# Two transformer blocks on one core: the first block's gating products, weight halves and conv taps in another order

## The chip, the cores and the metric

The kernel runs on one core of a Trainium2 chip. The metric is the time of one execution on the device in microseconds (us). A core has TensorE (PE in the profile; its weight loads are PEld), VectorE (DVE), ScalarE (ACT), GpSimd (POOL) and SyncE (SP), which here issues the loads of weights. Each engine takes its instructions in the order in which they are written; semaphores join the engines.

## The reference

The input is 1024 tokens of 1024 values, float32. The first block, which the change concerns:

```python
h = rms_norm(x, norm1_g)
u_a, v_a, val_b, gate_b = split(h @ w_in)                  # 4 x 512 columns
v = layer_norm(gelu(v_a)).reshape(1, 8, 128, 4, 128)
mixed = einsum('hts,bcshd->bcthd', tril(sgu_w), v) + sgu_b
a_out = gelu(u_a) * mixed
g = val_b * sigmoid(gate_b)
c = causal depthwise conv of g, 31 taps, + conv_b
b_out = silu(layer_norm(c in 4 groups of 128))
x = x + concat(a_out, b_out) @ w_out
h = rms_norm(x, norm2_g)
x = x + square(relu(h @ w_ff1)) @ w_ff2                    # 4096 wide
return rms_norm(x, final_g)
```

The second block follows: a layer of differential attention, a layer of stick-breaking attention, with their projections. It is the same before and after.

## The kernel before

**Products.** A float32 matrix becomes two float16 halves, a high one (value times a power of two, rounded) and a low one (what the rounding left). A product takes high by high, high by low and low by high: 24 matmuls of 128 x 512 for one bank of PSUM with a sum over 1024, 12 with a sum over 512. Weights come in 42 tiles of 2 MB. Tiles 0 to 3 are `w_in` (val, gate, v, u), 4 and 5 `w_out`, from 6 on the feed-forward layer. Tile i is loaded by SyncE into one raw buffer once tile i-1 is converted (`weight`). ScalarE adds up its absolute values (`total`), GpSimd takes the largest sum over the partitions, VectorE makes the power of two (`factor`, three small operations), ScalarE the high half, VectorE the low half (`convert_low`); `convert` on VectorE is `factor` and `convert_low` in a row, so VectorE waits out ScalarE's high half. Tile 0 takes its peak on VectorE.

**Order.** There is no scheduler: the functions `tensor`, `vector`, `scalar`, `gpsimd`, `sync` are each engine's program. The first block, in n = 0, 1 (halves of the tokens) and m = 0 to 3 (groups of 128 channels):

1. `tokens("ht")` turns the scaled input on TensorE, `tokens_high` and `tokens_low` split it; `tokens("xt")` turns the raw input into `XT`, the residual stream.
2. 16 products of val and gate: all val of n = 0, all gate of n = 0, then for each m val and gate of n = 1. `gate` is a Sigmoid on ScalarE, `glu` the multiplication on VectorE. A group of the convolution needs `glu` of both halves.
3. The convolution: `run_taps(k)` gives VectorE the next k of 120 taps of `taps_order`, each 128 x 1024, four chains of 30, with two chains alternating at first. It is called in portions between VectorE's other work.
4. 8 products v, 8 products u; `bn_stats`, then two passes over V; 8 `sgu` products (each a bias matmul with one row and four 128 x 128 matmuls in float32); VectorE multiplies them by gelu(u) and takes a peak of each half (`gated_peak`). GpSimd, then `power`, `gated_high` on ScalarE and `gated_low` on VectorE follow.
5. Part 0 of the output product (`out_part(0, ...)`, 16 of them, z = 0 to 15), each followed by `out_residual` on VectorE. Between them: `centre`, `centre_sums`, `centre_spread` (the group norm on TensorE), `centre_factor`, `mix_norm`, `mix_silu`, `mix_high`, `mix_lows`.
6. Part 1, 16 products over the convolution's channels; its first product needs group 3 to be through. Then the second norm and the feed-forward layer.

`mix_high` waits for the last tap of all, since its buffer `MH[1]` lies over the convolution's input `G`. In the profile one line stands for a helper: L72 matmul, L75 transpose, L81 activation, L84 copy on ScalarE, L90 copy, L93 `tensor_tensor`, L96 `tensor_scalar`, L101 `scalar_tensor_tensor` (taps, residuals, low halves), L110 reduction, L113 reciprocal, all on VectorE but for the first four.

## Time and profile before

| | us |
|---|---|
| median of 3 runs (2599.11 to 2602.09) | 2599.43 |
| the profiled execution | 2594.74 |
| its span, first to last instruction | 2592.9 |
| TensorE busy | 2361.3 |
| VectorE busy | 1543.2 |
| ScalarE busy | 953.7 |

A profile shows one execution. "Busy" adds up the time in which an engine works. The busy shares are means over the whole span; the first block fills only its first 439 us, which is where the change lies.

### The profile page before, as it was taken

Reading aid. Unit: us, or ns where it says so; the run is one execution under the profiler, and the core shown is the slowest. Engines: PE = TensorE matmul, PEld = TensorE weight load, DVE = VectorE, ACT = ScalarE, POOL = GpSimd, SP = SyncE. Lnnn points to the kernel's source line nnn. Section 1 sums busy time; section 2 is a strip of 40 time slices with the busy share of each in tenths; the row PEclk is TensorE's granted clock in tenths of the full one; section 3 lists DMA queues with packets and bytes.
Section 4 is the critical chain, followed back from the end, with each engine's and each line's share of the span. In section 5 each row is a group of like instructions: output and inputs, shape, how many; then the busy total and the mean of one; then the engine's idle time right before and its main releaser. Section 6 shows DMA issues by size and latency. Waiting matters only on the chain.

```text
span 2592.9 us, 30076 instructions
## 1 busy us (share of the span) xinstructions
PE 2361.3 (91%) x12784; PEld 1249.2 (48%) x12784; DVE 1543.2 (60%) x1979; ACT 953.7 (37%) x1346; POOL 208.2 (8%) x264
## 2 busy tenths in 40 slices
PE   6998659999999999898999967889999998888899
PEld 3444324444444444444444445664444445676764
DVE  5569885564445545577651278974644405988852
ACT  5232223321212212333322166761323214777741
POOL 0000002000000000333320201002000000000000
PEclk9997769999999999999999989999999998999999
DMA  4010000121111011103010000011140200000021
GB/s 172 33 65 33 33 0 1 66 80 51 46 52 65 33 65 38 56 8 130 33 65 33 33 1 1 1 66 65 33 162 14 84 1 33 1 1 1 1 82 49
DMA packets 50321, 115.99 MB, mean 45 GB/s; under 512 B 2384, under 2 KB 7817, under 8 KB 49804
## 3 DMA queue, kind: packets, MB, share of 16 engines
q1 hardware_dynamic: 48452, 105.39, 11.4%
q10 hardware_dynamic: 1736, 8.68, 0.8%
q8 instruction: 101, 1.65, 0.3%
q14 instruction: 32, 0.26, 0.0%
HBM read 101.49 MB, written 12.58 MB: 44 GB/s over the span
## 4 chain that ended last, share of the span: by engine, by line
PE 69%; DVE 19%; ACT 7%; issue 3%; DMA 1%; POOL 1%; SPq 0%; DVEq 0%; POOLq 0%; ACTq 0%
PE PS L72 66%; DVE R L101 7%; ACT RG L81 4%; PE PS L75 3%; DVE R L93 3%; DVE RG L101 2%; DVE RG L107 2%; DVE mx L110 2%; ACT R L81 1%; DVE scl L110 1%; ACT OV L84 1%; DMA RG<-in_a_w_in 1%; DVE RG L93 1%; DVE oss L110 1%; ACT OV L81 0%
## 5 line engine op out<-in xcount | busy, mean ns | idle before, releaser
L72 PE MATMUL PS<-R,RG 128*128 128x512 f16 (+1 forms) x5472 | 1173.0, 376 | 42.0 <-DVE R L101 29.9
L72 PEld LDWEIGHTS PS<-R,RG 128*128 128x128 f16 (+1 forms) x5472 | 544.2, 104 | 667.0 <-issue 58.7
L72 PE MATMUL PS<-RG,R 128*128 128x512 f16 x2880 | 634.2, 381 | 3.8 <-DVE R L101 3.8
L72 PEld LDWEIGHTS PS<-RG,R 128*128 128x128 f16 x2880 | 282.7, 98 | 337.0 <-issue 6.5
L81 ACT ACTIVATE R<-PS,scl 128x512 f32<-128x512 f32 (+1 forms) x200 | 131.0, 686 | 724.9 <-PE PS L72 601.5
L101 DVE SCALAR_TENSOR_TENSOR R<-PS,scl,R 128x512 f32<-128x512 f32 (+1 forms) x216 | 155.1, 746 | 178.4 <-PE PS L72 131.6
L72 PE MATMUL PS<-R,OV 128*128 128x64 f32 (+2 forms) x1456 | 194.4, 286 | 58.5 <-DVE R L93 31.7
L107 DVE TENSOR_TENSOR_SCAN RG<-RG 128x127 f32<-128x127 f32 (+7 forms) x128 | 168.6, 1345 | 108.9 <-ACT RG L81 108.3
L101 DVE SCALAR_TENSOR_TENSOR RG<-RG,scl 128x4096 f16<-128x4096 f32 x42 | 188.6, 4490 | 71.0 <-ACT RG L81 71.0
L72 PEld LDWEIGHTS PS<-R,OV 128*128 128x128 f32 x1456 | 180.6, 199 | 70.1 <-DVE R L93 38.5
L81 ACT ACTIVATE RG<-RG,scl 128x4096 f16<-128x4096 f32 x42 | 155.7, 3708 | 137.7 <-DVE scl L113 137.6
L75 PE MATMUL PS<-ident,RG 128*128 128x128 f32 x864 | 147.9, 288 | 49.6 <-ACT OV L84 23.9
L110 DVE TENSOR_REDUCE scl<-RG 128x1 f32<-128x4096 f32 x35 | 154.5, 4413 | 64.9 <-DMA RG<-in_a_w_in 24.9
L122 POOL PARTITION_ALL_REDUCE scl<-scl x63 | 33.6, 535 | 1752.9 <-DVE scl L110 1357.3
L81 ACT ACTIVATE RG<-PS,scl 128x1024 f32<-128x1024 f32 (+3 forms) x172 | 168.6, 982 | 0.9 <-PE PS L72 0.9
L104 DVE CUSTOM_DVE_ANT_0 R<-R 128x512 f32<-128x512 f32 (+1 forms) x66 | 44.3, 676 | 181.1 <-ACT R L81 180.9
L101 DVE SCALAR_TENSOR_TENSOR R<-R,OV 128x1024 f32<-128x1024 f32 x120 | 150.7, 1279 | 1.9
L84 ACT COPY OV<-PS 128x512 f32<-128x512 f32 (+3 forms) x215 | 110.9, 516 | 106.0 <-PE PS L75 102.0
L72 PE MATMUL PS<-R 64*128 64x512 f16 (+3 forms) x1152 | 124.9, 343 | 22.3 <-ACT RG L81 20.4
L75 PEld LDWEIGHTS PS<-ident,RG 128*128 128x128 f32 x864 | 102.5, 153 | 63.1 <-DVE RG L101 26.6
L81 ACT ACTIVATE RG<-PS,mx,scl 128x128 f32<-128x128 f32 (+7 forms) x128 | 106.0, 839 | 41.8 <-DVE mx L96 41.2
L93 DVE TENSOR_TENSOR R<-PS,R 128x512 f32<-128x512 f32 (+1 forms) x96 | 64.7, 683 | 71.2 <-ACT R L81 46.0
(109 smaller groups left out, 1538.9 us busy)
## 6 DMA issues: line engine op xcount, KB each, us to landing
RG<-in_w_ff SPq DMA_DIRECT2D x16, 2048.0 KB, 8.1
RG<-in_a_w_in SPq DMA_DIRECT2D x8, 2048.0 KB, 8.7
RG<-in_w_in SPq DMA_DIRECT2D x4, 2048.0 KB, 10.0
xspill<-R ACTq DMA_DIRECT2D x2, 4096.0 KB, 16.3
RG<-in_w_kv SPq DMA_DIRECT2D x4, 2048.0 KB, 8.4
RG<-in_b_w_in SPq DMA_DIRECT2D x4, 2048.0 KB, 8.0
R<-in_x SPq DMA_DIRECT2D x8, 512.0 KB, 9.6
RG<-in_w_out SPq DMA_DIRECT2D x2, 2048.0 KB, 7.7
```

The lines of the kernel that those rows point to most:

```text
L72: return self.engine.matmul(*a, **k) if self.engine else Nothing()
L75: return self.engine.transpose(*a) if self.engine else Nothing()
L81: return self.engine.activation(*a, **k) if self.engine else Nothing()
L84: return self.engine.copy(*a) if self.engine else Nothing()
L93: return self.engine.tensor_tensor(*a) if self.engine else Nothing()
L101: return self.engine.scalar_tensor_tensor(out=out, in0=in0, scalar=scalar, in1=in1, op0=op0, op1=op1)
L104: return self.engine.tensor_tensor_reduce(*a) if self.engine else Nothing()
L107: return self.engine.tensor_tensor_scan(*a) if self.engine else Nothing()
L110: return self.engine.tensor_reduce(*a, **k) if self.engine else Nothing()
L122: return self.engine.partition_all_reduce(*a) if self.engine else Nothing()
```

## The change

Eight edits, all in the first block:

- **First tile by halves.** Tile 0's high and low half are each made in two pieces of 2048 columns (`first_high`, `first_low`), between the splits of the tokens; the first product starts on the first piece (`by_half`). `factor(0)` moves ahead of three splits.
- **Group by group.** For each m: gate of n = 0, val of n = 1, gate of n = 1, `glu` of both, then taps. `tokens_raw(0)` moves behind the 16 products, on ScalarE alone; `tokens_raw(1)` and `tokens_scaled(1)` move forward. The Sigmoid's output lies in two other buffers.
- **Factor apart from the low half.** For tiles 1 to 6 `factor(i)` stands some taps or splits ahead of `convert_low(i)`.
- **Taps.** Chain 1 starts after 10 taps of chain 0 instead of 6. 29 taps stand before the v products' statistics (20 before), 50 before the last statistics (42), 65 before the gating multiplications (70), and one tap follows each of the first six of these.
- **Gated scale from sums.** Two reductions on VectorE are replaced by eight `Abs` passes with a sum on ScalarE; one factor serves both halves.
- **Centring earlier.** `centre(0)` and `centre(1)` stand ahead of the output products, `centre(2)` at z = 12.
- **Buffers.** `MH[1]` lies in R2, the squares in R0, and `mix_high` of groups 0 to 2 no longer waits for the last tap.
- `total` writes its unused output into a slot of the weights and waits for that slot.

TensorE, start of the program; L75 are transposes, 128x124 turns the taps, RG holds weights:

```order
-L75 MATMUL PS<-ident,R 128x128 x64
+L75 MATMUL PS<-ident,R 128x128 x32
 L72 MATMUL PS<-R,RG 128x512 x48
 L75 MATMUL PS<-ident,R 128x128 x32
-L72 MATMUL PS<-R,RG 128x512 x72
-L75 MATMUL PS<-ident,R 128x128 x32
-L72 MATMUL PS<-R,RG 128x512 x96
+L72 MATMUL PS<-R,RG 128x512 x24
+L75 MATMUL PS<-ident,R 128x128 x16
+L72 MATMUL PS<-R,RG 128x512 x24
+L75 MATMUL PS<-ident,R 128x128 x16
+L72 MATMUL PS<-R,RG 128x512 x24
```

The raw input's first half (32 transposes) has left the place ahead of the first product.

VectorE, the gating stage; `PS,scl,dg` and `PS,scl,OV` are `glu` of n = 0 and 1, 128x1024 the taps:

```order
+L101 SCALAR_TENSOR_TENSOR R<-PS,scl,dg 128x512 [waits s_bank_act,s_w_scale]
 L90 COPY OV<-PS 128x124 [waits s_bank_full]
-L101 SCALAR_TENSOR_TENSOR R<-PS,scl,R 128x512 [waits s_bank_act,s_bank_dve]
+L101 SCALAR_TENSOR_TENSOR R<-PS,scl,OV 128x512 [waits s_bank_full,s_bank_act,s_bank_dve]
+L96 TENSOR_SCALAR R<-R,OV,cols 128x1024 [waits s_glu]
+L101 SCALAR_TENSOR_TENSOR R<-R,OV 128x1024 [waits s_conv_dve] x3
+L101 SCALAR_TENSOR_TENSOR R<-PS,scl,dg 128x512 [waits s_bank_act]
+L101 SCALAR_TENSOR_TENSOR R<-R,OV 128x1024 [waits s_conv_dve] x7
+L96 TENSOR_SCALAR scl<-scl 128x1 [waits s_w_top]
```

The first tap now stands behind the second `glu`, where before three more `glu` stood ahead of it.

TensorE, behind the last `sgu` product; `R,OV` is centring, `ones,R` sums of squares, `OV,ones` the spread:

```order
-L72 MATMUL PS<-R,RG 128x512 x24
 L72 MATMUL PS<-R,OV 128x512 x4
-L72 MATMUL PS<-R,RG 128x512 x48
-L72 MATMUL PS<-ones,R 128x1 x16
+L72 MATMUL PS<-ones,R 128x1 x8
+L72 MATMUL PS<-R,RG 128x512 x12
+L72 MATMUL PS<-ones,R 128x1 x8
 L72 MATMUL PS<-R,RG 128x512 x36
 L72 MATMUL PS<-OV,ones 128x512 x2
 L72 MATMUL PS<-R,RG 128x512 x24
 L72 MATMUL PS<-OV,ones 128x512 x2
-L72 MATMUL PS<-R,RG 128x512 x60
```

Centring of two groups now comes first; one output product stands between the two groups of sums.

The diff, cut to what the prediction speaks of:

```diff
-        sgt = R2[:, 0:1024].rearrange("p (a n) -> p a n", a=2)
+        sgt = [dg[:, :, :].rearrange("p t q -> p (t q)"), OV[:, 1024:1536]]
...
-        SQC = R2[:, 0:4096].rearrange("p (m n) -> p m n", m=4)
-        MH = [R3[:, 4096 * i:4096 * i + 4096].bitcast(F16).rearrange("p (s k n) -> p s k n", s=2, k=4)
-              for i in range(2)]
+        SQC = R0[:, 0:4096].rearrange("p (m n) -> p m n", m=4)
+        gated_abs = R0[:, 4096:8192].rearrange("p (j n) -> p j n", j=8)
+        gated_sums = mx[:, 16:24]
+        MH = [a.bitcast(F16).rearrange("p (s k n) -> p s k n", s=2, k=4) for a in (R3[:, 0:4096], R2[:, 0:4096])]
+        SQ3 = R3[:, 4096:8192].rearrange("p (k n) -> p k n", k=8)
...
-        taps_order = ([(0, w) for w in range(1, 7)]
-                      + [(m, w) for w in range(1, TAPS - 6) for m, w in ((0, w + 6), (1, w))]
-                      + [(1, w) for w in range(TAPS - 6, TAPS)]
+        taps_order = ([(0, w) for w in range(1, 11)]
+                      + [(m, w) for w in range(1, TAPS - 10) for m, w in ((0, w + 10), (1, w))]
+                      + [(1, w) for w in range(TAPS - 10, TAPS)]
...
+                e.wait_ge(*(sig("weight").at(i, 0) if by_half else sig("weight").at(i)))
...
+                    if by_half and k == 4:
+                        e.wait_ge(*sig("weight").at(i))
...
             tokens_scaled(0)
-            tokens_raw(0)
+            product_t(0, 0, 0, h_rhs, ("val", 0, 0), 0, ready=h_ready("norm1", 0), by_half=True)
+            product_t(0, 1, 0, h_rhs, ("val", 1, 0), 1)
+            tokens_scaled(1)
+            product_t(0, 2, 0, h_rhs, ("val", 2, 0), 2)
+            tokens_raw(1, range(4))
+            product_t(0, 3, 0, h_rhs, ("val", 3, 0), 3)
+            tokens_raw(1, range(4, 8))
+            places = [(4, 5, 6), (7, 0, 4), (5, 1, 6), (7, 2, 0)]
             for m in range(4):
-                if m == 2:
-                    tokens_scaled(1)
-                product_t(0, m, 0, h_rhs, ("val", m, 0), m, ready=h_ready("norm1", 0))
-            for m in range(4):
-                if m == 1:
-                    tokens_raw(1)
-                product_t(1, m, 0, h_rhs, ("gate", m, 0), 4 + m % 2)
-            for m in range(4):
-                product_t(0, m, 1, h_rhs, ("val", m, 1), ready=h_ready("norm1", 1))
+                product_t(1, m, 0, h_rhs, ("gate", m, 0), places[m][0])
                 if m == 0:
...
                     e.transpose(b[:, 0:124], taps_t, ident[0:124, 0:124]).then_inc(*full.up("taps"))
-                product_t(1, m, 1, h_rhs, ("gate", m, 1))
...
+                product_t(0, m, 1, h_rhs, ("val", m, 1), places[m][1], ready=h_ready("norm1", 1))
+                product_t(1, m, 1, h_rhs, ("gate", m, 1), places[m][2])
+            for c in range(3):
...
+            tokens_raw(0)
...
+            centre(0)
+            centre(1)
+            centre_sums(0)
             for z, (n, c, mi) in enumerate(out_order):
-                if z == 2:
-                    centre(0)
-                    centre(1)
+                if z == 1:
+                    centre_sums(1)
+                if z == 4:
+                    centre_spread(0)
                 if z == 6:
-                    centre_sums(0)
-                    centre_sums(1)
-                if z == 9:
-                    centre_spread(0)
-                if z == 11:
                     centre_spread(1)
+                if z == 12:
+                    centre(2)
+                if z == 14:
+                    centre_sums(2)
                 out_part(0, n, c, mi)
-            for mi in (2, 3):
-                centre(mi)
-                centre_sums(mi)
-                centre_spread(mi)
+            centre_spread(2)
+            centre(3)
+            centre_sums(3)
+            centre_spread(3)
...
+            def first_low(j):
+                e.wait_ge(*sig("w_high").at(0, j))
+                s, a = w_slot(0), 2048 * j
+                low_half(s[:, a:a + 2048], s[:, 4096 + a:6144 + a], w_raw(0)[:, a:a + 2048], w_col(0, 2)).then_inc(
+                    *(sig("weight").up(0) if j else sig("weight").up(0, 0)))
...
-            for k in range(4):
+            tokens_low(0, 0)
+            factor(0)
+            tokens_low(0, 1)
+            tokens_low(0, 2)
+            first_low(0)
+            tokens_low(0, 3)
+            tokens_low(0, 4)
+            first_low(1)
+            for k in range(5, 8):
                 tokens_low(0, k)
-            e.wait_ge(*sig("w_top").at(0))
-            power(w_inv(0), w_col(0, 2), w_col(0, 1)).then_inc(*sig("w_factor").up(0))
-            for k in range(4, 8):
-                tokens_low(0, k)
-            convert_low(0)
-            tokens_raw(0)
             tokens_scale(1)
             h_scale(0, "norm1")
-            for k in range(8):
+            for k in range(3):
                 tokens_low(1, k)
-            convert(1)
+            factor(1)
+            for k in range(3, 8):
+                tokens_low(1, k)
+            convert_low(1)
...
             for m in range(4):
                 glu(m, 0)
...
-                if m == 2:
-                    convert(2)
-                    h_scale(2, "norm1")
-            for m in range(4):
                 if m == 0:
                     e.wait_ge(*full.at("taps"))
...
+                if m == 2:
+                    run_taps(1)
+                    convert_low(2)
+                    h_scale(2, "norm1")
+                if m:
+                    run_taps(3 if m == 2 else 7)
+                if m == 1:
+                    factor(2)
                 glu(m, 1)
...
-                run_taps(5)
+                run_taps(2 if m == 3 else 3)
...
+            for t in range(NT):
+                run_taps(0 if t == 3 else 3)
+                if t == 1:
+                    factor(3)
+                if t == 3:
+                    convert_low(3)
+                    h_scale(3, "norm1")
+                if t == 7:
+                    factor(4)
+                if t:
+                    v_stats(t - 1)
+            v_stats(NT - 1)
+            for t in range(NT):
...
+            run_taps(10)
+            factor(5)
+            run_taps(4)
+            convert_low(5)
+            run_taps(1)
...
-            for n in range(2):
-                e.wait_ge(*sig("bank_dve").at("sgu", 3, n))
-                e.tensor_reduce(col(86 + n), MIX[:, 0:4, cols512(n)], AX.XY, ALU.max,
-                                apply_absolute_value=True).then_inc(*sig("gated_peak").up(n))
-            run_taps(2)
-            for n in range(2):
-                e.wait_ge(*sig("gated_top").at(n))
-                power(col(57 + n), col(92 + n), col(90 + n)).then_inc(*sig("gated_factor").up(n))
-            for n in range(2):
-                run_taps(2)
+                    run_taps(1 if h < 3 else 0)
+            run_taps(1)
...
             for z, (n, c, mi) in enumerate(out_order):
-                if z == 3:
-                    convert(6)
+                if z == 0:
+                    gated_lows(1)
+                if z == 2:
+                    centre_factor(0)
+                if z == 4:
+                    mix_norm(0)
+                    centre_factor(1)
+                if z == 5:
+                    factor(6)
+                if z == 6:
+                    mix_norm(1)
                 if z == 8:
-                    centre_factor(0)
+                    convert_low(6)
                 if z == 10:
-                    centre_factor(1)
+                    mix_lows(0)
                 if z == 11:
-                    mix_norm(0)
-                if z == 13:
-                    mix_norm(1)
-                if mi == 0:
-                    out_scale(0, n, c)
+                    mix_lows(1)
+                if mi == 0 and n == 0:
+                    out_scale(0, c)
                 out_residual(0, n, c, mi)
-                run_taps(1 if z in (3, 8, 10, 11, 13) else 2 if z % 2 else 1)
-            run_taps(max(0, 98 - taken[0]))
+                run_taps(0 if z in (2, 4, 6, 8) else 1)
+                if z == 11:
+                    run_taps(max(0, 90 - taken[0]))
             centre_factor(2)
             run_taps(4)
             mix_norm(2)
+            run_taps(6)
+            mix_lows(2)
...
+                if i == 2:
+                    e.wait_ge(*sig("weight").at(1))
+                if 3 <= i < 7:
+                    e.wait_ge(*full.at(*last_product.get(i - 3, ())))
+                out = R3[:, 0:2048].bitcast(F16) if i == 7 else w_slot(i)[:, 0:4096]
...
+            for h in range(4):
+                for n in range(2):
+                    e.wait_ge(*sig("bank_dve").at("sgu", h, n))
+                    e.activation(gated_abs[:, 2 * h + n, :], MIX[:, h, cols512(n)], ACT.Abs,
+                                 accum_out=gated_sums[:, 2 * h + n:2 * h + n + 1]).then_inc(*sig("gated_sum").up(h, n))
...
-            convert(6)
             centre(0)
+            gated_highs(0)
             centre(1)
+            gated_highs(1)
             centre_root(0)
             centre_root(1)
+            total(6)
             mix_silu(0)
+            mix_high(0)
+            convert(6)
             mix_silu(1)
-            centre(2)
-            centre_root(2)
-            mix_silu(2)
-            for mi in range(3):
+            mix_high(1)
+            for mi in (2, 3):
+                centre(mi)
+                centre_root(mi)
+                mix_silu(mi)
                 mix_high(mi)
```

## Rows read from the trace of the kernel before

**Rows 1.** Page part 2: busy tenths of 40 slices of 64.8 us

```profile
PE   6998659999999999898999967889999998888899
PEclk9997769999999999999999989999999998999999
```

**Rows 2.** By stretch: us, busy us of each engine (instructions), clock, DMA

```profile
core 0: us, PE busy (x) PEld busy (x) DVE busy (x) ACT busy (x) POOL busy (x), PEclk, DMA share, GB/s
...
35.00:135.49 100.49, 98.74 (x460) 46.62 (x460) 49.18 (x64) 25.54 (x27) 0.80 (x2) 0.97 0.09 34
135.49:218.46 82.97, 82.97 (x385) 37.46 (x383) 66.04 (x93) 31.31 (x26) 1.82 (x3) 1.00 0.15 51
218.46:249.40 30.94, 29.01 (x81) 16.64 (x80) 26.77 (x24) 10.31 (x8) 0.71 (x1) 0.56 0.19 68
...
277.40:341.90 64.50, 60.81 (x260) 29.51 (x260) 53.70 (x61) 16.93 (x22) 0.00 (x0) 0.92 0.09 33
...
373.90:390.60 16.70, 13.99 (x34) 7.04 (x34) 7.77 (x14) 11.61 (x18) 0.00 (x0) 0.54 0.00 0
```

**Rows 3.** The same view, VectorE alone, up to its last tap

```profile
103.00:264.60 161.60, 130.26 (x154) 0.86 0.11 39
264.60:373.90 109.30, 97.54 (x103) 0.75 0.06 20
```

**Rows 4.** Timeline, ScalarE: start us, busy us, engine line operation operands count

```profile
22.59 3.71 ACT L81 ACTIVATE RG<-RG,scl 128x4096 f16<-128x4096 f32 x1
```

**Rows 5.** Timeline, VectorE, up to its gating products and peaks

```profile
19.39 2.72 DVE L101 SCALAR_TENSOR_TENSOR R<-PS,cols,R 128x512 f16<-128x512 f32 x4
...
26.34 4.48 DVE L101 SCALAR_TENSOR_TENSOR RG<-RG,scl 128x4096 f16<-128x4096 f32 x1 [1.16 <-ACT RG L81]
...
126.72 6.06 DVE L101 SCALAR_TENSOR_TENSOR R<-R,OV 128x1024 f32<-128x1024 f32 x5
...
246.68 13.17 DVE L101 SCALAR_TENSOR_TENSOR R<-R,OV 128x1024 f32<-128x1024 f32 x10
259.77 4.87 DVE L93 TENSOR_TENSOR R<-PS,R 128x512 f32<-128x512 f32 x8
264.55 4.47 DVE L110 TENSOR_REDUCE scl<-R 128x1 f32<-128x2048 f32 x2
```

**Rows 6.** Timeline, TensorE, up to the first output products

```profile
35.01 11.86 PE L72 MATMUL PS<-R,RG 128*128 128x512 f16 x48 [9.12 <-ACT R L84]
46.71 1.91 PE L75 MATMUL PS<-ident,R 128*128 128x128 f32 x16
48.87 2.63 PE L75 MATMUL PS<-ident,R 128*128 128x128 f32 x16 [0.26 <-DVE R L101]
...
67.38 1.04 PE L75 MATMUL PS<-ident,R 128*128 128x128 f32 x8
68.65 4.08 PE L75 MATMUL PS<-ident,R 128*128 128x128 f32 x24 [0.24 <-ACT R L84]
...
218.46 1.12 PE L72 MATMUL PS<-OV,ones 1*128 1x512 f32 x2
219.51 1.16 PE L72 MATMUL PS<-OV,R 128*128 128x128 f32 x8
...
277.46 6.63 PE L72 MATMUL PS<-R,RG 128*128 128x512 f16 x24 [28.07 <-DVE R L101]
```

**Rows 7.** Timeline, TensorE: sums of squares and centring beside the output products

```profile
297.72 4.21 PE L72 MATMUL PS<-ones,R 128*128 128x1 f32 x32
...
373.97 3.78 PE L72 MATMUL PS<-R,OV 128*128 128x512 f32 x4 [26.82 <-DVE R L101]
```

**Rows 8.** Granted clock around a restart of TensorE, two stretches of four us

```profile
277.00:281.00 4.00, 3.54 (x11) 1.41 (x12) 3.96 (x5) 0.00 (x0) 0.00 (x0) 0.61 0.00 0
281.00:285.00 4.00, 4.00 (x18) 1.94 (x17) 3.96 (x7) 0.00 (x0) 0.00 (x0) 1.00 0.00 0
```

**Rows 9.** Timeline, ScalarE: four high halves of the gated part

```profile
272.02 4.27 ACT L81 ACTIVATE R<-R,scl 128x1024 f16<-128x1024 f32 x4 [26.72 <-DVE scl L113]
```

230 lines of the change are left out of this document (110 added, 120 removed).

## The prediction

> **What bounds the kernel now.** I read the page's slices first: TensorE stands at nine tenths but for the first seven slices and a few of the second block's, where its granted clock falls too [rows 1]. So the first 439 us are the place, and behind them TensorE is full: what is won before passes through. Then the view by stretches [rows 2]: TensorE is full from the first product at 35.0 to the end of the u products at 218.5; in the `sgu` products it is full at 0.56 of its clock; then it stands 28.1 us until the first output product [rows 6] and again 26.8 us before the last centring [rows 7]. Both waits end on VectorE's L101. From 103.0, about its first tap, to its last tap at 373.9 VectorE has 31.3 us idle up to the end of gating at 264.6 and 11.8 us behind it [rows 3]. The chain therefore runs: TensorE to 135, VectorE's taps from there to 373.9, and a tail of 16.7 us over centring, spread and split until part 1 runs full at 390.6 [rows 2]. I take it stage by stage: when does TensorE get there, when VectorE, and which is later.
>
> **Stage 1, to the v products.** Before, the factor of tile 0 is ready at 22.55, ScalarE's half takes 3.71, the low half 4.48 and ends at 30.8; TensorE starts only at 35.01, after a copy of the raw input has freed its bank [rows 4 to 6]. Now one split instead of four stands ahead of the factor, three times 0.68 less: 20.6. Half a high half (1.9) and half a low half (2.25) give 24.8. The product's second half waits: one split and the second piece on ScalarE end at 25.0, two splits on VectorE at 26.2, the second low piece at 28.4, three more splits at 30.5, the last three matmuls at 31.1. Before, the first product ended at 35.01 + 11.86/2 = 40.9: 9.8 earlier. The other 94.6 us of the way to 135.5 stay, with two edits: the raw first half is turned here, 32 transposes at 1.91/16, plus 3.8 (before it was free, in the wait for the weights); the raw second half took from 67.4 to 72.7 in two banks and takes 3.8 in four, minus 1.5; some 1 us of small waits goes. v starts at 31.1 + 94.6 + 3.8 - 1.5 - 1.0 = 127.0, 8.5 earlier.
>
> **Stage 2, to the end of gating.** v and u take 83.0 as before, to 210.0. The eight `sgu` products took 30.9 with one wait of 1.9 [rows 2]: 29.0, to 239.0, and the last multiplication (0.61) ends at 239.6. VectorE: the gate of group 0 is done on both halves after seven products, not ten, so taps start at 31.1 + 6 x 5.2 (82.97/16 [rows 2]) + 4.6 (the turning before went from 46.9 to 51.5 [rows 6]) + 3.8 + 0.3 + 1.4 (Sigmoid and `glu`, each 0.7 like a split) = 72.4, say 73. Its work from there was 130.3 with 70 taps and 8 multiplications; now 71 taps, plus what used to lie ahead of 103: three `glu` (0.7 each), tile 2 (4.48 and a factor of 0.5) and three copies (0.7 each): 130.3 + 1.3 + 2.1 + 5.0 + 2.1 = 140.8. One new wait: the exponential for lambda stands on ScalarE behind the eight copies and `total(3)`, some 5 us (an estimate: a pass over a tile takes 3.7, and eight copies of 0.5 stand ahead). VectorE would be through at 219. TensorE is later by 20 us, so it sets 239.6; before it was VectorE, at 264.6. 25.0 won, of which 20 of VectorE's waits have only moved into the `sgu` products. In front of the waiting multiplication stands every tap behind it, which is why they count.
>
> **Stage 3, gated split.** The two reductions (4.47), one factor (0.5) and two scales (0.3) go. The last `Abs` (a 512-wide pass, half of 4.27/4 and a little for its sum) lies beside taps. ScalarE then has `centre(0)` (four passes, 2 us) ahead of the high halves (4.27/4 each) [rows 9], so VectorE waits about 2.3. The first output product starts at 246.5: 6.9 us behind gating, against 277.5 - 264.6 = 12.9 before.
>
> **Stage 4, output products and the last taps.** VectorE's work from 264.6 to 373.9 was 97.5. Now: minus 5.3 (stage 3), minus one tap (1.3), plus six low halves of groups 0 to 2 that used to stand behind the last tap (4 x 1.0), plus 0.1: 95.0. Its waits: 2.3 (stage 3); z = 0 to 7 run at TensorE's pace, 8 x 2.6 (half a full product) + 2.1 (sums, half of 4.21 [rows 7]) + 2 x 1.9 (spread, as wide as half of a centring) = 26.7 against VectorE's 20 (8 residuals of 0.7, two low halves, five taps, two spreads' factors and norms): about 8 with the skew; and at z = 12 a new one: TensorE waits for tap 90 before `centre(2)`, VectorE's next step is the residual of z = 12. After a hole of some 12 us centring takes 3.78 [rows 7] and the product about 3 (the restart at 277 had 0.61 of the clock in its first 4 us, 1.00 in the next [rows 8]), then 2.5 and 0.6 around the sums: 10. Together 20.3, against 11.8 before. The last tap ends at 239.6 + 95.0 + 20.3 = 354.9.
>
> Here a rule of the Trainium skill can be weighed. Taps of one chain in a row take 13.17/10 = 1.32 each, of alternating chains 6.06/5 = 1.21 [rows 5]. The change has 40 alternating taps instead of 48, which by the rows costs 8 x 0.1 = 0.9. "VectorE: DVE Perf Modes", section "The DRAIN you can't avoid", says that a semaphore between two operations costs nothing extra since the pipeline empties anyway; by that the order of chains is worth 0. The rows disagree by 0.1 a tap, and I keep the 0.9.
>
> **Stage 5, tail.** 16.7, minus 0.4 because the six high halves of groups 0 to 2 no longer stand before `centre(3)` on ScalarE. What is late next there is TensorE at half clock (0.54 [rows 2]), unchanged. Part 1 runs full at 354.9 + 0.9 + 16.3 = 372.1 instead of 390.6: 18.5 won. Behind it nothing is changed but addresses.
>
> **Unknown costs.** The clock of the small pieces between the output products: 277.4 to 341.9 ran at 0.92; the new order has more holes. Between nothing (0) and the whole stretch's products at the low level for a further 8% (4): I take 2. The sums' `Abs` beside VectorE's work and its addresses: 0 to 1, below it -1, since one factor serves both halves; 0. The 24.8: the factor, now ahead of three splits, may find GpSimd's answer late; those splits took 2.0, so 0 to 2; the peak is ready at 19.4 and one split still stands ahead, so 0. Total 18.5 - 2 = 16.5. The sum against the profiled execution, 2594.7, gives 2578.2. The median of the runs is 4.7 above that execution; the same difference is kept: 2599.4 - 16.5 = 2583.
>
> **Rivals.**
> A, nothing comes through (within 0.2%, about 5 us, what a measurement of this kernel can tell from no change): the taps are the same 120 and VectorE's waits only move, as 20 us do into the `sgu` products. It needs the waits of stage 4 to be 33 instead of 20, for instance 0.8 more per output product. For it: VectorE waited before in the same places [rows 3]. Against: the work behind gating is less. 2596.
>
> B, slower: the clock. In the `sgu` products the granted clock is 0.56, for most of the stretch the low level of 1.2 GHz. TensorE now goes on with short centring matmuls and sums with holes between them, not into 28 us of rest and a dense restart. Should it stay low through part 0, each of 16 products takes 5.2 instead of 2.6 and VectorE behind them waits for it: up to 16 x 2.6 = 42, 36 of it on the chain, so 2599.4 - 16.5 + 36 = 2619. It decides for slower from the seventh product at the low level. Against: the restart at 277.5 was at full clock four us later [rows 8], and the stretch of 277.4 to 341.9, with centring, sums and spreads among its products, ran at 0.92 [rows 2].
>
> C, more: the low clock of `sgu` doesn't come. At the level of its first product, 1.12 + 1.16 [rows 6], the high one, eight take 18.2 instead of 29.0; then gating ends at 229 and ten more come through: 2573. Against: TensorE was full for 83 us before it and the clock fell all the same; the order of these matmuls is unchanged.
>
> D, half: stage 1 stalls. Bank after bank is freed by VectorE and ScalarE in the new interleaving, and a late copy or `total(2)` in front of a Sigmoid holds back TensorE. If v starts at 133 instead of 127, gating ends 6 later and the gain is 10: 2589. For it: 16 products with a dozen hand-overs.
>
> **Numbers.** Forecast (a gain of 12 to 20) 0.58; A 0.10, B 0.05, C 0.09, D 0.18. Range: C's end to A's edge, 2574 to 2595; the forecast's own range is 2579 to 2588. Faster by over 0.2% (below 2594): forecast, C, D and a part of what lies beside them, 0.87; same 0.08; slower 0.05.
>
> **What would show it.** First product at about 25, first tap at about 73, v at 127, end of the `sgu` products at 239, first output product at 246.5, last tap at 355, part 1 full at 372. VectorE's idle time moves from 135 to 182 into 220 to 239 and behind z = 11. The forecast is wrong if `sgu` runs at full clock, if the output products stay at the low one, or if VectorE reaches gating later than TensorE.

## The result and the profile after

The changed kernel takes 2573.4 us (median of four runs, 2569.0 to 2576.8), the kernel before in the same comparison 2599.3. The ratio is 0.9898 with a 95% interval of 0.988 to 0.9917: 25.9 us are gained, by the interval 22 to 31. Forecast were 2583 us and a gain of 16.5. The direction and the places were right; the gain was put 9 us too small, and 2573.4 lies just below the range, 2574 to 2595.

The profiled execution of the changed kernel took 2576.8 us, its span is 2575.0. First the busy tenths of the page's 40 slices:

```profile
PE   6999649999999999898999877899999998888899
PEclk9997869999999999899999999999999998999999
```

Beside [rows 1] the fourth slice is fuller (9 for 8) and the sixth emptier (4 for 5). The view by stretches, cut at the stages of this kernel (columns as in [rows 2]), and VectorE alone:

```profile
core 0: us, PE busy (x) PEld busy (x) DVE busy (x) ACT busy (x) POOL busy (x), PEclk, DMA share, GB/s
73.00:127.50 54.50, 54.02 (x254) 27.10 (x253) 50.05 (x55) 14.99 (x17) 0.85 (x1) 0.97 0.11 39
127.50:210.50 83.00, 83.00 (x385) 37.50 (x385) 76.13 (x95) 38.20 (x31) 1.60 (x3) 1.00 0.14 51
210.50:239.60 29.10, 29.10 (x82) 17.10 (x82) 14.20 (x15) 5.75 (x15) 0.00 (x0) 0.56 0.21 73
246.20:311.00 64.80, 49.25 (x222) 23.84 (x223) 49.30 (x56) 24.30 (x28) 0.35 (x1) 0.87 0.09 33
354.30:365.00 10.70, 8.94 (x24) 4.42 (x25) 2.19 (x4) 5.69 (x8) 0.00 (x0) 0.66 0.00 0
```

```profile
73.00:240.30 167.30, 141.06 (x166) 0.91 0.14 51
240.30:354.30 114.00, 95.81 (x101) 0.78 0.05 19
```

VectorE's work is near the forecast: 141.1 us up to the end of gating (forecast 140.8) and 95.8 behind it (95.0). Now TensorE's timeline (start us, busy us, engine, line, operation, operands, count, idle time before), whose rows answer to [rows 6] and [rows 7]:

```profile
25.08 12.22 PE L72 MATMUL PS<-R,RG 128*128 128x512 f16 x48 [4.16 <-DVE RG L101]
...
246.24 2.75 PE L72 MATMUL PS<-R,RG 128*128 128x512 f16 x12 [0.69 <-DVE R L101]
...
298.12 3.78 PE L72 MATMUL PS<-R,OV 128*128 128x512 f32 x4 [15.51 <-DVE R L101]
...
354.35 3.40 PE L72 MATMUL PS<-R,OV 128*128 128x512 f32 x4 [35.11 <-DVE R L101]
357.69 1.02 PE L72 MATMUL PS<-ones,R 128*128 128x1 f32 x8
...
417.07 1.05 PE L72 MATMUL PS<-ones,R 128*128 128x1 f32 x8 [1.79 <-POOL R L93]
```

The first product starts 9.9 us earlier, the first output product 31.2, the last centring 19.6. The last row is a wait for GpSimd that stands in the kernel before too, at 439.38; behind it both programs do the same, so I take it as the mark of what the first block gained: 22.3 us in this pair of executions.

VectorE's timeline shows where its waits have gone:

```profile
132.98 0.15 DVE L96 TENSOR_SCALAR lamt<-lamt 128x1 f32<-128x1 f32 x1 [7.24 <-ACT lamt L81]
...
215.56 0.69 DVE L93 TENSOR_TENSOR R<-PS,R 128x512 f32<-128x512 f32 x1 [0.98 <-PE PS L72]
219.57 0.69 DVE L93 TENSOR_TENSOR R<-PS,R 128x512 f32<-128x512 f32 x1 [2.12 <-PE PS L72]
...
239.60 0.69 DVE L93 TENSOR_TENSOR R<-PS,R 128x512 f32<-128x512 f32 x1 [3.31 <-PE PS L72]
...
304.96 0.75 DVE L101 SCALAR_TENSOR_TENSOR R<-PS,scl,R 128x512 f32<-128x512 f32 x1 [6.89 <-PE PS L72]
...
311.84 0.75 DVE L101 SCALAR_TENSOR_TENSOR R<-PS,scl,R 128x512 f32<-128x512 f32 x1 [2.23 <-PE PS L72]
314.43 0.75 DVE L101 SCALAR_TENSOR_TENSOR R<-PS,scl,R 128x512 f32<-128x512 f32 x1 [0.65 <-PE PS L72]
```

In [rows 5] the eight multiplications stand in one row without a wait, since VectorE came last. Now all but the first wait for their bank: TensorE sets the end of gating, at 240.3 instead of 264.6. The three waits behind z = 12 add up to 9.8.

A table of the marks that I use below, in us. "Sgu high" is how many of the eight groups of gating products had the high clock; "out" is the output product and "last tap" its end; "POOL wait" is the start of the row behind the wait for GpSimd; "rest" is the span less that mark.

```
execution        sgu high  sgu start-end   first out  last tap  POOL wait  rest
before           2         218.5-249.4     277.5      373.9     439.4      2153.5
before_again     3         218.9-249.8     277.9      376.1     440.1      2158.0
after            2         210.5-239.6     246.2      354.3     417.1      2157.9
again            5         210.4-234.1     241.0      349.6     412.3      2154.5
whole_tile0      2         217.2-246.4     253.0      361.0     424.9      2156.2
late_centre      2         208.9-237.9     244.5      342.6     405.4      2157.7
more_taps        4         211.8-237.4     244.0      342.8     405.5      2150.6
late_and_more    2         211.2-240.4     247.1      336.4     399.2      2155.5
reduce_peak      2         211.1-240.4     251.3      361.4     424.2      2154.2
late_mix_high    2         210.3-239.3     246.0      349.9     413.9      2157.2
no_bias          -         210.2-217.5     230.5      340.6     403.4      2157.4
before_no_bias   -         219.2-236.8     278.5      376.7     440.8      2154.1
lambda_early     2         210.4-239.7     246.4      354.3     418.2      2156.3
split_bias_all   8         210.3-223.3     236.3      329.9     392.8      2151.2
```

### The profile page after: what moved, and what is told of

Its sections match the earlier page's. It is cut to its first block, busy times and chain, and to the rows that moved or that the text cites. A ratio compares the mean times of both kernels' runs of the same rounds, so it can differ in the third digit from the quotient of the medians.

```text
span 2575.0 us, 30098 instructions
## 1 busy us (share of the span) xinstructions
PE 2354.4 (91%) x12784; PEld 1249.0 (49%) x12784; DVE 1537.0 (60%) x1970; ACT 963.0 (37%) x1367; POOL 206.9 (8%) x263
## 4 chain that ended last, share of the span: by engine, by line
PE 74%; DVE 15%; ACT 6%; issue 3%; POOL 1%; DMA 1%; ACTq 0%; DVEq 0%; POOLq 0%
PE PS L72 71%; DVE R L101 4%; PE PS L75 4%; ACT RG L81 3%; DVE R L93 2%; DVE RG L107 2%; DVE mx L110 2%; DVE RG L101 1%; ACT OV L84 1%; DVE scl L110 1%; DMA RG<-in_a_w_in 1%; DVE RG L93 1%; ACT R L81 1%; DVE oss L110 1%; ACT OV L81 0%
## 5 line engine op out<-in xcount | busy, mean ns | idle before, releaser
L101 DVE SCALAR_TENSOR_TENSOR R<-PS,scl,R 128x512 f32<-128x512 f32 (+1 forms) x208 | 149.0, 746 | 164.2 <-PE PS L72 140.2
L101 DVE SCALAR_TENSOR_TENSOR RG<-RG,scl 128x4096 f16<-128x4096 f32 (+1 forms) x43 | 188.7, 4388 | 50.3 <-ACT RG L81 50.3
L75 PE MATMUL PS<-ident,RG 128*128 128x128 f32 x864 | 150.5, 292 | 51.6 <-DVE RG L101 24.1
L81 ACT ACTIVATE RG<-RG,scl 128x4096 f16<-128x4096 f32 (+1 forms) x43 | 156.0, 3629 | 97.5 <-DVE scl L113 97.5
L75 PEld LDWEIGHTS PS<-ident,RG 128*128 128x128 f32 x864 | 104.3, 155 | 65.2 <-DVE RG L101 28.3
L93 DVE TENSOR_TENSOR R<-PS,R 128x512 f32<-128x512 f32 (+1 forms) x96 | 65.4, 684 | 86.5 <-ACT R L81 46.0
```

What stands on the lines that cost most here:

```text
L75: return self.engine.transpose(*a) if self.engine else Nothing()
L81: return self.engine.activation(*a, **k) if self.engine else Nothing()
L93: return self.engine.tensor_tensor(*a) if self.engine else Nothing()
L101: return self.engine.scalar_tensor_tensor(out=out, in0=in0, scalar=scalar, in1=in1, op0=op0, op1=op1)
```

## The experiments

All are edits of the changed kernel but for the two whose names begin with "before". The edits are shown shortened: most have a counterpart in another engine's program that is not printed. Each was timed in five rounds. Medians and ratios are against the kernel before, whose median was 2598.6, 2598.9 and 2599.6 in the three comparisons.

**The changed kernel again.**

> The changed kernel as it is, timed again with a new profile. In the first pair of profiles the changed kernel is 22.3 us ahead when TensorE waits for GpSimd's last square (439.4 before, 417.1 after), but its whole span is only 17.9 shorter, and the medians lie 25.9 apart. Theory 1, the change's gain is made in the first block alone and the rest differs from execution to execution: the wait for GpSimd's last square again ends at 417 within 0.5, the time behind it lies anywhere between 2150 and 2158, and the ratio of the medians comes nearer to 22 us (0.9915). Theory 2, the earlier start changes something behind the first block as well: the time behind it is on one side of 2153.5 by the same amount again, and the ratio stays at 0.990 or below.

2569.3 us, ratio 0.9897 (0.988 to 0.9914), 29.3 below its kernel before. Neither theory held whole: the rest, 2154.5, lies in the range of the first, but the POOL wait came at 412.3 and not at 417, and the ratio stayed where the second had it. Its profile differs from the first one in the gating products. Five of the pairs of bias matmuls take 1.12 us and three 2.07, where in the first profile two took 1.12:

```profile
218.94 1.12 PE L72 MATMUL PS<-OV,ones 1*128 1x512 f32 x2
219.99 2.07 PE L72 MATMUL PS<-OV,R 128*128 128x128 f32 x8
221.99 2.07 PE L72 MATMUL PS<-OV,ones 1*128 1x512 f32 x2
...
240.98 2.75 PE L72 MATMUL PS<-R,RG 128*128 128x512 f16 x12 [0.23 <-DVE R L101]
```

A matmul of the same kind takes 1.85 times as long from here on: the granted clock has gone from the high level (2.4 GHz) to the low one (1.2 GHz), with TensorE at work without a pause before it. The second profile of the kernel before (before_again) shows another case: three groups are at the high level, and behind a wait of 4.34 us for ScalarE all is at the low one.

```profile
229.74 2.07 PE L72 MATMUL PS<-OV,ones 1*128 1x512 f32 x2 [4.34 <-ACT R L81]
```

The moment differs between executions of one program. Three groups more at the high level put the first output product 5.3 us earlier and the last tap 4.7.

**The first tile whole again.**

```
-            tokens_low(0, 0); factor(0); tokens_low(0, 1); tokens_low(0, 2); first_low(0)
-            tokens_low(0, 3); tokens_low(0, 4); first_low(1); tokens_low(0, 5..7)
+            tokens_low(0, 0..3); factor(0); tokens_low(0, 4..7); convert_low(0)
```

> Tile 0 is converted whole again, after all eight splits, as before the change; all else as changed. Theory 1, TensorE's count of work from its first product sets the end of gating: first product at about 31 instead of 25.1, but without the stall inside the first product (6.4 instead of 5.9 there), so v products at 127.5 + 5 = 133, the end of gating and the last tap 5 later, time +5 us against the changed kernel. Rival, VectorE's taps set the end of gating and stage 1 is hidden: the start of v moves by 5 and the time by under 1.

2580.5 us, ratio 0.993 (0.9913 to 0.9947). One of its six runs took 6239.8 us and says nothing of the kernel; the median of the other five is 2578.1. The first product starts 5.8 us later, the v products and the last tap 6.7 each and the POOL wait 7.9:

```profile
30.86 13.14 PE L72 MATMUL PS<-R,RG 128*128 128x512 f16 x48 [10.06 <-DVE RG L101]
```

So the halves are worth 6.7 us (5 were expected), and start-up time comes through in full. The last 1.2 of the 7.9 are chance: the sums of squares in the tail ran at the low clock here (3.41 for 16, against 1.02 and 1.05 for two times 8).

**Centring behind the output products.**

```
-                if z == 12: centre(2)
-                if z == 14: centre_sums(2)
                 out_part(0, n, c, mi)
+            centre(2); centre_sums(2)      (behind the loop)
```

> Centring of group 2 and its sums are moved on TensorE from z = 12 and 14 to behind z = 15; VectorE is unchanged. Theory 1, TensorE waits at z = 12 for tap 90 while VectorE's next step is the residual of z = 12, and VectorE's idle time of 6.9, 2.2 and 0.7 us there lies on the chain of taps: it goes, the four output products run under the nine taps, last tap some 6 us earlier (the factor of group 2 then waits some 4 for centring and sums), time 5 to 7 us less than the changed kernel. Rival, that idle time is given back later, at the factor of group 2: the last tap moves by under 1.

2565.3 us, ratio 0.9872 (0.9854 to 0.9889). TensorE's row at z = 12 and what became of it:

```profile
265.21 26.06 PE L72 MATMUL PS<-R,RG 128*128 128x512 f16 x120
296.42 3.78 PE L72 MATMUL PS<-R,OV 128*128 128x512 f32 x4 [5.15 <-DVE R L101]
```

The output products run through to 291, and VectorE's residuals find them done. From the first output product to the last tap it takes 98.1 us instead of 108.1: the waits behind z = 12 cost 10, as the prediction had it (some 6 were expected for this edit), and are not needed.

**More taps in the gating gaps.**

```
-                    run_taps(1 if h < 3 else 0)
+                    run_taps(0 if (h, n) == (3, 1) else 1 if h + n == 0 else 2)
```

> 13 taps instead of 6 between the eight gating multiplications (none of the 120 is added, the filling at z = 11 shrinks from 8 to 1). Theory 1, TensorE sets the pace of the gating multiplications at half clock (4.0 each) and VectorE's 2.1 us of idle before each are free: gating still ends at 240.2, tap 90 comes 9 us earlier, last tap and time 8 to 9 us less than the changed kernel. Rival, the waits are not free, the multiplications fall behind TensorE: gating ends by up to 7 us later and the time stays within 1.

2559.6 us, ratio 0.9864 (0.9845 to 0.9883). The first output product stays (244.0, with four groups at the high clock), the last tap comes 9.3 us nearer to it (98.8 instead of 108.1), since seven taps now stand in VectorE's waits. In this profiled execution the rest, 2150.6, is the shortest of all, so its whole time would credit the edit with more than it did.

**Both together.**

> Both of the last two edits: centring of group 2 behind z = 15, and 13 taps between the gating multiplications. Measured apart, against the changed kernel at the same end of gating, the last tap came 10.0 us (late centring) and 9.3 us (more taps) earlier. Theory 1, they take different waits away (VectorE's at z = 12 to 15, VectorE's in the gating stage) and add up but for what the shrunken filling no longer hides: with the filling at z = 11 down to 1 tap, TensorE reaches the output products z = 12 to 15 only just ahead of VectorE, so 2 to 4 us of the waits stay: last tap about 16 us earlier than in the changed kernel, some 97 + (16 - 10) x -1 = 92 us behind the first output product (108.0 in the changed kernel). Rival, both have taken the same wait: last tap no more than 11 us earlier (97 behind).

2556.0 us, ratio 0.9837 (0.9821 to 0.9852). From the first output product to the last tap 89.3 (92 were expected): the two gains nearly add up (10.0 + 9.3 = 19.3, measured 18.8). By the medians it is 13 to 17 us faster than the changed kernel (2569.3 and 2573.4). Its waits at the multiplications are down to 0.80:

```profile
224.40 0.69 DVE L93 TENSOR_TENSOR R<-PS,R 128x512 f32<-128x512 f32 x1 [0.81 <-PE PS L72]
228.41 0.69 DVE L93 TENSOR_TENSOR R<-PS,R 128x512 f32<-128x512 f32 x1 [0.80 <-PE PS L72]
```

**The peak by a reduction again.**

```
-    ScalarE: eight Abs passes with a sum, one behind each multiplication
-    VectorE: tensor_reduce(col(86), gated_sums, ...)             128 x 8
+    VectorE: tensor_reduce(col(86), MIX[:, 0:4, :], ...)         128 x 4096
```

> The gated scale from a reduction on VectorE again (one of 128 x 4096), without the eight passes of ScalarE; the factor stays one for both halves. Theory 1, the reduction (4.4) lies on VectorE's chain behind gating with nothing to hide it: first output product 4.2 later behind the end of gating (6.0 in the changed kernel, now some 10.2), last tap and time 4 us later. Rival, the passes on ScalarE delayed it as much as they saved: under 1 us.

2580.6 us, ratio 0.993 (0.9916 to 0.9944). The reduction stands between the last multiplication and the first output product:

```profile
251.26 4.71 PE L72 MATMUL PS<-R,RG 128*128 128x512 f16 x12 [5.09 <-DVE R L101]
```

```profile
242.22 4.41 DVE L110 TENSOR_REDUCE scl<-R 128x1 f32<-128x4096 f32 x1
```

The first output product is 5.0 later than in the first profile and the last tap 7.1. Of both, 0.8 is not the edit's: the gating products end at 240.4 here and at 239.6 there. So the reduction costs 4.2 at the first output product, as expected, and some 2 more behind it, which are the first product itself: behind 5.1 us of rest it takes 4.71 instead of 2.75. The expectation, 4 in all, had left these out; the sums are worth 6.3 us.

**High and low halves of the gated groups late again.**

```
-            mix_silu(0); mix_high(0); convert(6); mix_silu(1); mix_high(1)
-            for mi in (2, 3): centre; centre_root; mix_silu; mix_high
+            mix_silu(0); convert(6); mix_silu(1); centre(2); centre_root(2); mix_silu(2)
+            mix_high(0..2); centre(3); centre_root(3); mix_silu(3); mix_high(3)
(VectorE: mix_lows(0..2) behind the last tap in place of z = 10, z = 11 and run_taps(6))
```

> The high halves of the convolution's groups 0 to 2 wait for the last tap again, and their low halves stand behind it on VectorE, as before the change; the buffers stay as changed. Theory 1, six low halves (4.1) leave VectorE's way to the last tap, which comes 4 us earlier, and lie beside TensorE's centring of group 3; but the six high halves (3.8) stand before ScalarE's reading of that centring, so the way from last tap to the full part 1 is 16.6 as before instead of 13.9: time 1.4 less than the changed kernel, within what can be told from it. Rival, the change's gain came from here: the time is 3 us or more above the changed kernel.

2571.6 us, ratio 0.9894 (0.9879 to 0.9909), not to be told from the changed kernel. The trace has two effects, one against the other:

```profile
349.96 3.78 PE L72 MATMUL PS<-R,OV 128*128 128x512 f32 x4 [33.90 <-DVE R L101]
354.91 1.93 PE L72 MATMUL PS<-ones,R 128*128 128x1 f32 x16 [1.17 <-ACT R L81]
358.33 3.78 PE L72 MATMUL PS<-OV,ones 128*128 128x512 f32 x4 [1.49 <-DVE OV L93]
```

The sums follow 4.95 us behind the centring, as in the kernel before, where the changed kernel has 3.34: ScalarE's six high halves stand ahead of its squares again, and the tail from last tap to POOL wait is 64.0 instead of 62.8. But VectorE's six low halves (4.07) now lie beside the centring instead of ahead of the last tap, which is 103.9 behind the first output product instead of 108.1. The POOL wait comes 3.1 earlier, too little for these medians to show. By this pair of traces the early halves of the changed kernel cost more (4.2) than they gave (1.2).

**The gating products without their bias.** The bias is left out of the result.

```
-                    e.matmul(b, ones[0:1, :], bsK[0:1, 128 * h:...], start=True, stop=True)
...
-                        mm = e.matmul(..., sguK[:, h, :], start=False, ...)
+                        mm = e.matmul(..., sguK[:, h, :], start=True, ...)
```

> The gating products leave out their bias matmul (one row, 128 x 512, float32, 2 passes of 1.0 at half clock); the added bias is left out of the result. Theory 1, TensorE sets the end of gating: its eight products then take 8 x 2.1 = 17 us at half clock or 9 at full clock instead of 24 to 29, VectorE becomes the later one there (its multiplications and taps, 1.9 each: gating ends some 15 us behind its first multiplication at 212.7, so at 227 to 228 instead of 235 to 240), time 8 to 12 us less. Also told apart: whether the one-row matmuls make the granted clock fall (it then stays at 1.0 through the stage) or something else (it falls all the same). Rival, VectorE sets the end of gating anyway: under 2 us.

2559.2 us, ratio 0.9845 (0.9829 to 0.986).

```profile
210.18 7.31 PE L72 MATMUL PS<-OV,R 128*128 128x128 f32 x64
...
226.39 3.54 PE L72 MATMUL PS<-ones,R 128*128 128x1 f32 x16 [5.46 <-ACT R L81]
230.45 4.69 PE L72 MATMUL PS<-R,RG 128*128 128x512 f16 x12 [0.52 <-DVE R L101]
```

The 32 matmuls of 128x128x128 take 7.3 us in float32 and run at 1.00 of the clock (the trace shows each of them as two, hence x64); with the eight one-row matmuls of the bias the same stretch takes 29. VectorE goes through its multiplications without a wait and ends them at 224.5 (227 to 228 were expected):

```profile
223.23 1.28 DVE L93 TENSOR_TENSOR R<-PS,R 128x512 f32<-128x512 f32 x2
```

The first output product stands 15.8 earlier than in the first profile and the last tap 13.7.

**The same in the kernel before.**

> The kernel before, without the two-term bias matmul of each spatial gating product (the bias is left out of the result, and nothing else). In the changed kernel the same edit took 12 to 14 us off, because there TensorE's products set when the gating multiplications are done. Theory: in the kernel before VectorE sets it. Its five rows from 228.69 to 259.77 us (one conversion and 21 taps) stand ahead of the multiplications without a wait for TensorE, which ends its last product at 249.4. So TensorE done 23 us earlier changes nothing: last multiplication at 264.6 as before, first output product about 277.5, last tap about 373.9, time within 3 us of the kernel before. Rival: the bias matmuls cost time wherever they stand (by the clock they leave behind, or by PSUM), and the kernel before gets 8 to 14 us faster too.

2598.4 us, ratio 1.0001 (0.9988 to 1.0014): nothing. TensorE ends the gating products 12.5 us earlier (236.8), and VectorE does not notice:

```profile
230.31 6.54 PE L72 MATMUL PS<-OV,R 128*128 128x128 f32 x40 [8.17 <-ACT R L81]
```

```profile
247.70 13.17 DVE L101 SCALAR_TENSOR_TENSOR R<-R,OV 128x1024 f32<-128x1024 f32 x10
260.79 4.87 DVE L93 TENSOR_TENSOR R<-PS,R 128x512 f32<-128x512 f32 x8
```

One edit, 10 to 14 us on one side of the change (against its two medians) and none on the other. That shows that the change moved the bound of gating from VectorE to TensorE. The last tap, at 376.7, is near where before_again has it (376.1).

**Lambda early.**

```
-            total(3)
             e.wait_ge(*sig("lambda_sums").at()); e.activation(lamt[:, 2:4], ..., ACT.Exp)
+            total(3)
(VectorE: run_taps(3) ahead of its wait for lambda_exp instead of at t = 0 behind it)
```

> The changed kernel, with the lambda exponential on ScalarE ahead of total(3), and three of VectorE's taps ahead of its wait for it (they are taken from those behind it, so the number before gating is the same). This takes away VectorE's wait of 7.24 us at 132.98. Theory: nothing is gained, since VectorE's 7 us are spent in front of the gating multiplications instead: TensorE starts the gating products at 210.4 in both, and sets when they are done. Last multiplication 234 to 240, first output product 241 to 246, last tap 349.6 to 354.3, time within 3 us of 2569 to 2573. Rival: VectorE's load sets the stretch, and each us that it gets earlier comes through to the last tap: 344 to 347 and a time of 2562 to 2567.

2574.1 us, ratio 0.9905 (0.9891 to 0.9918): nothing. The wait of 7.24 is gone, and the last tap stands at 354.3 as before. But the 7 us did not move into the waits at the multiplications, as was expected. VectorE gives most of them back earlier, above all where it waits for ScalarE's copy of the last v product:

```profile
169.83 0.69 DVE L116 BATCH_NORM_STATS2 oss<-R 128x6 f32<-128x512 f32 x1 [4.02 <-ACT R L81]
```

Its conversion ahead of the multiplications starts only 0.8 earlier (206.2 against 207.1), so this run says little of who sets the end of gating.

**Everything together, with the bias in two bfloat16 rows.** A complete version.

```
+   late_centre, lambda_early
-            run_taps(1)                                     (behind convert_low(5))
+            run_taps(6)
-   bsK = the bias row, float32
+   bsK[:, 0:512] = bias in bfloat16; bsK[:, 512:1024] = bias - bsK[:, 0:512] in bfloat16
-   e.matmul(b, ones[0:1, :], bsK row, start=True, stop=True)
+   for s in range(2): e.matmul(b, bfloat16 view of ones, bsK half s, start=(s == 0), ...)
```

> The version that the runs so far point to, and a complete one: (1) both centre() steps of the third convolution tile stand behind the last output product, as in late_centre; (2) the lambda exponential early, as in lambda_early; (3) the bias of the gating products is held as the sum of two bfloat16 rows and added by two matmuls of 16 bits in place of one of float32; (4) six taps in place of one between the last conversion and the first gating multiplication, where VectorE would wait for TensorE. Theory: TensorE starts the gating products at 208.9 and needs 10 to 13 us for them instead of 24 to 29, so the first output product stands at 228 to 232 (230.45 where the bias was left out), and VectorE has fewer taps left behind it: last tap 325 to 332, POOL wait 388 to 395, time 2541 to 2550. Rival: TensorE's clock is lower behind so short a gating stretch, or VectorE arrives late at the multiplications for its five more taps, and the last tap stands at 335 to 340 as in late_and_more: 2553 to 2558.

2549.5 us (2545.9 to 2551.4), ratio 0.9808 (0.9793 to 0.9822): the fastest of all, 20 to 24 us ahead of the changed kernel's two medians.

```profile
210.30 0.60 PE L72 MATMUL PS<-OV,ones 1*128 1x512 bf16 x2
210.83 1.16 PE L72 MATMUL PS<-OV,R 128*128 128x128 f32 x8
...
236.25 5.02 PE L72 MATMUL PS<-R,RG 128*128 128x512 f16 x12 [0.52 <-DVE R L101]
```

The two bfloat16 matmuls take 0.60 where the one in float32 took 1.12 at the same clock, and all eight groups stay at the high level: 13.0 us instead of 29. The first output product came later than I expected (236.3 against 228 to 232), since VectorE has five more taps and is now the late one at the multiplications, as the rival said; those taps are not lost, and the last of all ends at 329.9, within 325 to 332.

**The kernel before again.**

> The kernel before once more, for a second profiled execution. The changed kernel's two executions differ by 5.3 us at the first output product (246.24 and 240.98), by how many groups of the float32 gating products ran at the lower clock. Theory: in the kernel before this does not reach the output products, since VectorE sets the end of gating: first output product 277.0 to 278.0 and last tap 373.4 to 374.4 again, whatever the gating products take (their end may be anywhere from 242 to 250). What is behind the POOL wait at 439.4 takes 2153 to 2158, which spreads the time by itself. Rival: the first output product moves by over 2 us with the gating products' end.

2598.8 us, ratio 0.9999 (0.9983 to 1.0015). The first output product is at 277.9, as expected. The last tap, at 376.1, is 1.7 later than I allowed; the first spread between the output products waited 1.4 longer for VectorE. The tail is shorter by 1.4, and the POOL wait is at 440.1 (first profile 439.4). The rest differs by 4.5 us.

## Why the gain was larger than forecast

No mechanism of the prediction failed; terms of its sum had the wrong size. Two of them cannot be put down to chance: the 0.4 of stage 5 for ScalarE's way in the tail, which is 1.2 by experiment, and the allowance for the clock between the output products, 2 where the trace shows 0. The duration of the gating products, stage 2, was taken as fixed and is not. Against the prediction's marks, in its own steps:

**Stage 1 was right.** Forecast 24.8 for the first product, 73 for the first tap and 127.0 for v; the trace has 25.08, 73.5 and 127.49. whole_tile0 shows the cause.

**Stage 2 was right in which engine, and took as fixed what isn't.** VectorE's 140.8 and the last multiplication at 239.6 against 141.1 and 239.60 to 240.3 in the first profile. That TensorE now sets the end of gating is shown by no_bias beside before_no_bias. By no_bias VectorE alone would be through at 224.5, not at 219, which did no harm. But the step "The eight `sgu` products took 30.9 with one wait of 1.9 [rows 2]: 29.0" is one execution's duration. Of the changed kernel's two profiles one has 29.1 and one 23.7. That is a part of rival C: the low clock comes, only later. The two mean 243.6 for the first output product instead of 246.5, 2.9 us more gained. Among eleven profiled executions with the float32 bias the count of groups at the high clock is 2 in eight cases, and 3, 4 and 5 in one each. So the first profile is the common case, and there the first output product is only 0.3 ahead of the forecast. In the kernel before the same swing was harmless, since VectorE set the end; what releases it I did not find out.

**Stage 3 was right to 1 us.** The first output product is at 246.24 against 246.5, because the last multiplication ended 0.7 late and the way behind it was 5.9 instead of 6.9. reduce_peak gives 4.2 for the reductions (4.47 in the prediction), with 2 more for a slow restart.

**Stage 4 was right, but for the allowance.** From the first output product to the last tap 108.4 were forecast, 108.1 and 108.6 measured, the waits behind z = 12 being 9.8 against 10. Two small errors met there: VectorE's work was 0.8 more, and its waits were 18.2 instead of 20.3, since the first eight output products cost it 5.2 instead of 8. The step "Between nothing (0) and the whole stretch's products at the low level for a further 8% (4): I take 2" was wrong: it is 0. The output products from 246.2 to 282.6 show no slow one; the granted clock of 0.87 over 246.2 to 311.0 is that of the hole ahead of z = 12 and what stands directly behind it:

```profile
246.20:282.60 36.40, 36.36 (x168) 17.33 (x168) 29.51 (x38) 19.29 (x21) 0.35 (x1) 1.00 0.08 25
282.60:298.10 15.50, 0.01 (x1) 0.00 (x0) 15.18 (x14) 0.00 (x0) 0.00 (x0) 0.60 0.20 79
```

**Stage 5 has the mis-sized term that the runs show.** "What is late next there is TensorE at half clock (0.54 [rows 2]), unchanged" failed. From the last tap to the POOL wait the kernel before took 65.4 (64.0 in its second profile), the changed one 62.8 and 62.7, not 65.0. Two things made it. ScalarE, free of six high halves, has the squares ready sooner, so that the sums stand 3.34 behind the centring instead of 4.95; late_mix_high put them back and got 4.95 and 64.0. I had this at 0.4; it is 1.2. ScalarE's first row behind the last tap, before and after:

```profile
374.03 3.79 ACT L81 ACTIVATE R<-R,scl 128x512 f16<-128x512 f32 x6 [22.81 <-DVE R L101]
...
356.46 0.58 ACT L84 COPY R<-PS 128x512 f32<-128x512 f32 x1 [30.12 <-PE PS L72]
```
The rest is the clock of the sums, 3.54 for 16 in the first profile of before against 1.93 in the second, so chance and no gain:

```profile
378.92 3.54 PE L72 MATMUL PS<-ones,R 128*128 128x1 f32 x16 [1.17 <-ACT R L81]
...
381.09 1.93 PE L72 MATMUL PS<-ones,R 128*128 128x1 f32 x16 [1.17 <-ACT R L81]
```

Part 1 starts at 365.05, in before at 387.36: 22.3 earlier, where 18.5 were forecast (my mark of 390.6 was the second row of that group, 3.2 later). The 0.9 for chained taps in the same line belongs nowhere near the tail: it would lie within the stages before, whose marks came out right without it.

Of taps in a row the changed kernel shows the same as [rows 5]: 21.09/16 = 1.32 for a chain, and three alternating ones 3.67/3 = 1.22.

```profile
99.94 3.67 DVE L101 SCALAR_TENSOR_TENSOR R<-R,OV 128x1024 f32<-128x1024 f32 x3
...
333.20 21.09 DVE L101 SCALAR_TENSOR_TENSOR R<-R,OV 128x1024 f32<-128x1024 f32 x16
```

The Trainium skill, "VectorE: DVE Perf Modes", section "The DRAIN you can't avoid", says that the next operation does not start until the pipeline is empty, adds that one which is not held starts earlier, and gives a measurement in which a semaphore between copies costs nothing. By that measurement the order of chains would make no difference; the trace disagrees by 0.1 us a tap, as before the change.

**The sum.** Over two profiles of each, the POOL wait is at 439.7 before and 414.7 after, 25.1 earlier; the rest means 2155.8 and 2156.2. That agrees with the 25.9 of the medians, less well with the 29.3 of the repeat, and the 17.9 between the first two spans is far off: one pair of executions was too little to compare by, since the rest alone ranges from 2150.6 to 2158.0 over 14 profiles of 12 programs that do the same there. The 8.6 between 25.1 and 16.5 are made of the earlier first output product (2.9), the last tap of the kernel before, which over two profiles is 1.1 later than in the first, the tail (62.7 against 64.7, so 2.0 instead of 0.4: 1.6), the allowance (2) and the 0.9. The 2.9 is mostly one execution's luck with the clock: with the first profile of the changed kernel alone the gain at the POOL wait is 22.7. What the medians show beyond that is not traced to a row.

Rivals A, B and D did not come: VectorE's waits behind gating are 18.2 us (114.0 less 95.8), not 33; no output product of the changed kernel ahead of z = 12 stood at the low clock; v started at 127.49, not 133. The median fell on rival C's number, 2573, but not by its mechanism: the low clock came in all eleven executions, and the terms above made up the sum.

## What to carry to other kernels

Ask at each meeting of two engines which comes last, and by how much: an edit of the other one is worth nothing until then (the bias matmuls, nothing before and 10 to 14 us after). A reordering that makes one engine early turns its time into waits at the next meeting, and these are the place for the following edit: independent work put into them, and the waiting step behind a loop instead of within it, took 18.8 us out of the way from the first output product to the last tap, and 13 to 17 us off the time. When a bound moves to an engine whose clock varies, the end of that stretch begins to vary with it (first output product 246.2 and 241.0 in two executions), and its duration in one profile is a sample, not a constant.

## What the runs showed of the hardware

A float32 matmul with one row is not cheap. One of 1x512 (two in the trace) takes 1.12 us at the high clock and 2.07 at the low one, as long as four full ones of 128x128x128 in the same type (1.16 and 2.08). With them among the gating products the granted clock fell to the low level within 3 to 11 us in all eleven executions, in ten of them with TensorE at work without a pause until then; without them (no_bias), or with the rows in bfloat16 (split_bias_all), it stayed at 1.00 for the whole stretch of 7 and 13 us:

```profile
210.30:223.10 12.80, 12.80 (x81) 8.56 (x81) 12.62 (x13) 2.66 (x6) 0.00 (x0) 1.00 0.46 165
```

Both stretches are shorter than 29 us, but the 13 are longer than any of the eleven took to fall. Still, it is one execution of each, so whether the kind of matmul saved the clock is left open. In the kernel before without the bias, 8.17 us of rest stand within the stretch, and the products behind it start at the low level.

A rest of TensorE costs twice: once as time at rest, once in the product that follows. Behind 0.7 us the first output product takes 2.75 us, behind 5.1 us 4.71, and in no_bias and split_bias_all, where 5.4 us of rest stand ahead of the sums in front of it, 4.69 and 5.02.
